# A two-layer streaming trunk on one core: the router of the second layer chooses before the norm's factor is known, the first gather is handed over in halves, the dense FFN waits by banks, and fifteen short products are added

## The chip, the cores and the metric

The kernel runs on one core of a Trainium2 chip. The metric is the device time of one execution in microseconds (us). TensorE multiplies, VectorE (DVE) and ScalarE (ACT) work element by element and prepare its operands, GpSimd (POOL) takes a small part in the recurrence, and SyncE (SP) issues nearly all DMAs.

## The reference

A trunk of two layers over 16 learned tokens and 256 frames of width 1024. Each layer runs three mixers in parallel on one projection, gates and merges them, multiplies by `w_out` and adds to the stream. Then comes an FFN on the normed stream: dense in layer 0, eight experts in layer 1.

```python
h = h + merged @ w_out[i]
hn = rms_norm(h, norm_ffn[i])
if i % 2 == 0:
    h = h + swiglu(hn, dense_w_gate[j], dense_w_up[j], dense_w_down[j])
else:
    h = h + moe_swiglu(hn, moe_router[j], moe_w_gate[j], moe_w_up[j], moe_w_down[j])

def moe_swiglu(x, router, wg, wu, wd):
    logits = (x @ router).astype(jnp.float32)
    top_val, top_idx = lax.top_k(logits, TOP_K)
    top_w = jax.nn.softmax(top_val, axis=-1)
    gates = jnp.sum(jax.nn.one_hot(top_idx, N_EXPERTS, dtype=jnp.float32) * top_w[..., None], axis=-2)
    y = jnp.zeros_like(x)
    for e in range(N_EXPERTS):
        y = y + gates[..., e:e + 1].astype(x.dtype) * swiglu(x, wg[e], wu[e], wd[e])
    return y
```

`rms_norm` divides each token's row by the root of its mean square. That factor is one positive number for all of a token's logits, so it doesn't change which two are largest; it scales their difference.

## The kernel before

**Layout and precision.** The stream is held transposed in `hT`, eight tiles of 128 features by T = 272 tokens. Most products are made in three parts: both operands are split into a high part, rounded to fp32r, and a low part, the difference. `three_products` (L538 to L540) adds high by high, low by high and high by low. ScalarE makes the high part of each half chunk of weights (`high_half`, L1350; `expert_high`, L1691: WH from ring), VectorE the low part (`low_half` and `expert_low`: WL, through the helper at L1776, which is the line of all its two-operand instructions). There are three buffers of each, used in turn. TensorE waits on `w_lo` for a half and counts it in `w_used` when done; ScalarE waits on `w_used` before it overwrites a buffer. SyncE loads chunks of 2 MB into a ring of three as `w_lo` frees them (`expert_loads`, L424).

**Order on the engines.** Each engine walks through a fixed list of halves. `split_stage` calls the splitting of a half and then the events that are written down for that place by `after_half(events, l, name, half)`. An engine carries out its list strictly in order, so an event that waits holds back the splits behind it.

**Norms.** `norm` on TensorE (L612) multiplies a matrix of ones by the squares, in three parts of 4, 2 and 2 feature tiles (`PARTS`), which ScalarE squares (L1355). VectorE makes the mean (L1790), ScalarE the root, VectorE the reciprocal (L1792) and the scaled `xn` (L1794). `keep_clock` (L603) issues ten products that nobody reads meanwhile.

**Dense FFN of layer 0.** Two blocks of hidden chunks, 0 to 3 and 4 to 6. For each chunk a gate product goes to PSUM banks 0 to 3 (`DG`) and an up product to banks 4 to 7 (`DU`). VectorE reads the gate banks into SF (`gate_scaled`, counts `f_g`) and the up banks into HF (`hidden`, counts `f_h`); after the block the down products (`DD`, `rows_half`) go to banks 0 to 7 and VectorE adds them to `hT` (`down`, `added`, L1776).

**From `w_out` to the experts.** The last two chunks of layer 1 before the experts are `O0` and `O1`, for banks 0 to 3 and 4 to 7, each in two halves (`columns_half`). VectorE adds the banks to `hT` (`added`), and makes the router's input in three parts: `router_input` (L1809) multiplies by the norm's gain alone. Between the halves of `O1` TensorE does part 0 of the sum of squares and `router_part(0)`: logits (L657) and transposes of the tokens (L663). After `O1` come the other parts. The reciprocal root is in a row; two products with one column turn it (L1189). Ten unread products follow (L1192). VectorE scales the logits (L2233), takes the two largest (`max`, `max_index`), makes one-hot rows of them (L2245), TensorE ranks the tokens for each expert (L1195 to L1199), VectorE makes slots (L2255, L2256) and the selection matrix of the first expert (L2373). ScalarE copies the turned tokens, scaled, into `hnT` (L1700), and makes the exponential for the gate weights (L1703). `gather` (L1207) multiplies the tokens by the selection, ScalarE copies the result into XGH (L1707), VectorE makes XGL from it, and `half_products` starts with the first half of the first expert. Each expert has 42 halves in a loop. The order is kept by the semaphores `router_pe`, `router_dve` and `router_act`, whose counts `ROUTER` names.

## Time and profile before

| | us |
|---|---|
| median of three runs | 2135.67 (2133.98 to 2139.07) |
| the profiled execution | 2132.18 |
| its span, first to last instruction | 2130.2 |
| TensorE busy | 2071.9 (97%) |
| VectorE busy | 1479.6 (69%) |
| ScalarE busy | 1230.9 (58%) |
| mean granted TensorE clock | 0.995 of full speed |

The stages in the trace: layer 0 up to about 380 us, its dense FFN up to 686, layer 1 up to 1106, the router up to 1125, the experts up to 2104, the last norm and the output. Durations of single instructions overlap on TensorE, because products are pipelined; what one costs in a stream is the time of many divided by their number. A full-precision product appears as two records, a rounded one (fp32r) as one.

### The profile page before, as it was taken

What the parts mean: (1) busy time and instruction counts of PE and PEld (TensorE: products, weight loads), DVE (VectorE), ACT (ScalarE), POOL (GpSimd) and SP (SyncE); (2) the same over time, 40 slices, a digit from 0 to 9 for tenths busy, and PEclk for the clock granted to TensorE, in tenths of its full rate; (3) what the DMA queues carried; (4) which work ended last, traced back from release to release, by engine and by line L of the source; (5) the groups of instructions that cost most, each with busy time, mean ns of one, the idle gap of its engine ahead of it and who ended that gap; (6) DMA issues with size and microseconds to landing.
All of it is one profiled execution on the core that took longest, in us unless ns stands there. A gap on an engine that the chain in (4) does not pass through costs nothing.

```text
span 2130.2 us, 35940 instructions
## 1 busy us (share of the span) xinstructions
PE 2071.9 (97%) x15200; PEld 1799.0 (84%) x15200; DVE 1479.6 (69%) x1340; ACT 1230.9 (58%) x1147; POOL 22.1 (1%) x24
## 2 busy tenths in 40 slices
PE   9999999999999999999999999999999999999997
PEld 7877789999999797788997888888888888888886
DVE  5633438565454673434848889898898989899886
ACT  4455445443333455445437777777777777777675
POOL 0000100000000000010000000000000000000000
PEclk9999999999999999999999999999999999999999
DMA  6323105444443232210637989899898989989894
GB/s 240 129 63 139 57 3 198 158 184 173 158 180 120 80 122 96 80 42 10 240 119 302 374 331 375 347 359 365 338 371 330 374 348 359 366 339 370 331 372 173
DMA packets 73981, 485.38 MB, mean 228 GB/s; under 512 B 12440, under 2 KB 13592, under 8 KB 16136
## 3 DMA queue, kind: packets, MB, share of 16 engines
q1 hardware_dynamic: 72584, 479.96, 58.3%
q10 hardware_dynamic: 1280, 3.70, 0.5%
q8 instruction: 94, 1.54, 0.3%
q14 instruction: 23, 0.19, 0.0%
HBM read 481.89 MB, written 1.74 MB: 227 GB/s over the span
## 4 chain that ended last, share of the span: by engine, by line
PE 91%; DVE 5%; ACT 2%; issue 1%; DVEq 0%; ACTq 0%
PE PS L538 24%; PE PS L540 23%; PE PS L539 23%; PE PS L943 5%; PE PS L809 2%; DVE area L1776 2%; PE PS L827 2%; PE PS L1207 1%; PE PS L1214 1%; PE PS L688 1%; DVE WL L1776 1%; PE PS L851 1%; ACT WH L1691 1%; PE PS L890 1%; PE PS L796 0%
## 5 line engine op out<-in xcount | busy, mean ns | idle before, releaser
L1776 DVE TENSOR_TENSOR WL<-ring,WH 128x2048 fp32r<-128x2048 f32 x410 | 934.2, 2289 | 218.1 <-ACT WH L1350 111.9
L1691 ACT ACTIVATE WH<-ring 128x2048 fp32r<-128x2048 f32 x336 | 643.0, 1916 | 156.9 <-PE PS L540 156.9
L538 PE MATMUL PS<-WH,XGH 128*128 128x512 f32 x896 | 353.5, 395 | 2.4 <-DVE XGL L1776 2.4
L540 PE MATMUL PS<-WL,XGH 128*128 128x512 f32 x896 | 349.6, 390 | 0.0
L539 PE MATMUL PS<-WH,XGL 128*128 128x512 f32 x896 | 349.1, 390 | 0.0
L540 PE MATMUL PS<-XL,WH 128*128 128x272 f32 (+1 forms) x704 | 202.6, 288 | 0.0
L1350 ACT ACTIVATE WH<-ring 128x2048 fp32r<-128x2048 f32 x74 | 141.1, 1910 | 104.3 <-PE PS L540 104.2
L538 PEld LDWEIGHTS PS<-WH,XGH 128*128 128x128 f32 x896 | 168.3, 188 | 36.3 <-DVE XGL L1776 2.6
L540 PEld LDWEIGHTS PS<-WL,XGH 128*128 128x128 f32 x896 | 168.2, 188 | 35.7
L539 PEld LDWEIGHTS PS<-WH,XGL 128*128 128x128 f32 x896 | 168.4, 188 | 33.5
L538 PE MATMUL PS<-WH,HTH 128*128 128x512 f32 x448 | 176.5, 394 | 0.6
L540 PE MATMUL PS<-WL,HTH 128*128 128x512 f32 x448 | 174.6, 390 | 0.0
L539 PE MATMUL PS<-WH,HTL 128*128 128x512 f32 x448 | 174.4, 389 | 0.0
L943 PE MATMUL PS<-area 64*64 64x64 f32 (+1 forms) x3680 | 129.1, 224 | 12.5 <-DVE area L1776 9.3
L943 PEld LDWEIGHTS PS<-area 64*64 64x64 f32 x3680 | 120.1, 135 | 20.3 <-DVE area L1776 13.6
L540 PEld LDWEIGHTS PS<-XL,WH 128*128 128x128 f32 x704 | 132.3, 188 | 0.0
L538 PE MATMUL PS<-FXH,WH 128*128 128x272 f32 x448 | 129.3, 289 | 2.3 <-DVE hT L1776 1.5
L539 PE MATMUL PS<-FXH,WL 128*128 128x272 f32 x448 | 128.8, 287 | 0.0
L1776 DVE TENSOR_TENSOR area<-PS,cst 128x256 f32<-128x256 f32 (+2 forms) x78 | 30.2, 404 | 122.6 <-PE PS L856 61.6
L538 PE MATMUL PS<-XH,WH 128*128 128x272 f32 (+1 forms) x384 | 109.7, 286 | 0.9 <-DVE ML L1776 0.4
L539 PE MATMUL PS<-XH,WL 128*128 128x272 f32 (+1 forms) x384 | 109.1, 284 | 0.0
L538 PEld LDWEIGHTS PS<-WH,HTH 128*128 128x128 f32 x448 | 84.1, 188 | 20.4 <-issue 3.7
(350 smaller groups left out, 3526.7 us busy)
## 6 DMA issues: line engine op xcount, KB each, us to landing
ring<-in_experts SPq DMA_DIRECT2D x336, 1024.0 KB, 6.6
ring<-in_weights SPq DMA_DIRECT2D x114, 1024.0 KB, 6.8
ring<-in_weights SPq DMA_DIRECT2D x4, 576.0 KB, 6.3
ring<-in_weights SPq DMA_DIRECT2D x4, 512.0 KB, 4.1
cst<-in_consts ACTq DMA_DIRECT2D x1, 1731.0 KB, 8.2
area<-in_x ACTq DMA_DIRECT2D x2, 512.0 KB, 4.7
out<-area SPq DMA_DIRECT2D x4, 256.0 KB, 2.1
bias_line<-lin SPq DMA_DIRECT2D x1, 672.0 KB
```

The lines of the kernel that those rows point to most:

```text
L538: pe.matmul(o, lh, rh, start=first, stop=False, skip_group_check=True)
L539: pe.matmul(o, ll, rh, start=False, stop=False, skip_group_check=True)
L540: return pe.matmul(o, lh, rl, start=False, stop=last, skip_group_check=True)
L688: ins = pe.matmul(PS[0:m, t % 4, 0:T], chunk_bufs[name][:, k, c:c + m], xn[:, k, 1:T + 1], start=(k == 0), stop=(k == KT - 1))
L809: ins = pe.matmul(PS[:, 6 + i % 2, 0:T], window_bufs[0][:, k, c:c + P], xn[:, k, 1:T + 1], start=(k == 0), stop=(k == KT - 1))
L827: ins = pe.matmul(PS[:, gate_bank(n), lo:T], early_bufs[0][:, k, (n % 4) * P:(n % 4 + 1) * P], xn[:, k, 1 + lo:T + 1], start=(k == 0), sto ...
L851: mm = lambda o, a, b_: pe.matmul(o, a, b_, start=False, stop=False, skip_group_check=True)
L890: ins = pe.matmul(PS[0:m, g, o:o + n], lhs, kC[r:r + 64, t0:t0 + n], start=True, stop=True)
L943: ins = pe.matmul(PS[r, bank, n * p + col:n * p + col + n], lhs[r, p], rhs(r, p), start=start if first is None else first and p == 0, stop ...
L1350: act.activation(WH[(g + 1) % 3][:, :], ring[b][:, 2048 * (g % 2):2048 * (g % 2) + 2048], ACT.Copy).then_inc(S("w_hi"), 1)
L1691: act.activation(WH[(BASE + j + 1) % 3][:, :], ring[b][:, 2048 * (j % 2):2048 * (j % 2) + 2048], ACT.Copy).then_inc(S("w_hi"), 1)
L1776: tt = lambda o, a_, b_, op: dve.tensor_tensor(o, a_, b_, op)
```

## The change

- **Short products.** In layer 1's first norm, ahead of the third part of the sum of squares, fifteen products of rounded operands (left from the dense FFN) with 96, 192 and 128 columns, five of each. Nobody reads their result.
- **Dense FFN.** The first down product of a block waits for `f_g` (banks 0 to 3 read), and only ahead of bank 4 for `f_h` (banks 4 to 7 read). The sum of the first block into `hT` starts with banks 0 to 3 on `f_mid`, which is counted after bank 3 of the block's last half.
- **Router.** The logits are compared unscaled. The squares are summed per token, as weights against one column of ones, so the mean is in a column without a turn. The order on TensorE is logits, squares, transposes by parts. The factor enters later, in the difference of the two largest logits. The ten unread products become two and three.
- **Splits.** The first two halves of the first expert are split under the halves of `O1`; the fill of the slots too.
- **First gather.** After its first four feature tiles TensorE counts `router_pe`; ScalarE and VectorE split the gathered tokens in two halves, and TensorE starts the first expert half, which needs only the first. Each expert's other products wait for `e_xgl` at their top.

`expert_high` and `expert_low` are moved up unchanged. In the diff line numbers are left out.

```diff
-        ROUTER = {"logits": 1, "turned": 2, "squares": 3, "rank": 4, "rstd": 1, "selected": 2, "gap": 3, "rows": 1, "exp": 2}
+        ROUTER = {"logits": 1, "squares": 2, "turned": 3, "rank": 4, "gathered": 5,
+                  "mean": 1, "selected": 2, "rstd": 3, "gap": 4, "rows_low": 5,
+                  "root": 1, "rows": 2, "exp": 3, "rows_high": 4}
...
             def norm(l, which, parts=(0, 1, 2), spare_products=10):
                 for i in parts:
+                    if (l, which, i) == (1, 0, 2):
+                        for n in (96, 192, 128):
+                            for _ in range(5):
+                                pe.matmul(PS[:, 1, 256:256 + n], FHH[:, 1, 0:P], FHH[:, 0, 0:n], start=True, stop=True)
                     if (l, which, i) == (0, 0, 0):
...
-            def router_part(q):
-
-                for i in PARTS_OF[q]:
-                    pe.wait_ge(S("hg_done"), i + 4)
...
+            def token_block(t):
+
+                return slice(META + t * P, META + (t + 1) * P)
+
+            def router_logits(i):
+
+                pe.wait_ge(S("hg_done"), i + 4)
+                for k in range(*PARTS[i]):
                     for t in range(2):
                         ins = pe.matmul(PS[:, 1, 8 * t:8 * t + 8], xn[:, k, 1 + META + t * P:1 + META + (t + 1) * P], router_sb[:, k, :],
                                         start=(k == 0 and t == 0), stop=(k == KT - 1), skip_group_check=True)
-                if q:
-                    ins.then_inc(S("router_pe"), 1)
+                return ins
+
+            def router_squares(i):
+
+                pe.wait_ge(S("sq_done"), part(DEPTH - 1, 1, i))
+                for k in range(*PARTS[i]):
+                    for t in range(2):
+                        ins = pe.matmul(PS[:, 0, t:t + 1], squares_of(DEPTH - 1, 1)[:, k, token_block(t)], C("ones", 0, 1),
+                                        start=(k == 0 and t == 0), stop=(k == KT - 1), skip_group_check=True)
+                return ins
...
+            def router_turns(i):
+
                 for t in range(2):
...
+                    for k in range(*PARTS[i]):
+                        ins = pe.transpose(PS[:, 2 + t + 2 * (k // 4), (k % 4) * P:(k % 4 + 1) * P],
+                                           xn[:, k, 1 + META + t * P:1 + META + (t + 1) * P], C("ident"))
+                return ins
...
                         if l and (h, half) == (1, 0):
-                            norm(l, 1, (0,))
-                            router_part(0)
-                if l:
-                    norm(l, 1, (1, 2), 0)
+                            router_logits(0)
+                            router_squares(0)
+                            router_turns(0)
...
                             pe.wait_ge(S("f_lo"), f + 1)
                             if f == block[0]:
-                                pe.wait_ge(S("f_h"), block[-1] + 1)
+                                pe.wait_ge(S("f_g"), block[-1] + 1)
+
+                            def before(d_):
+
+                                if f == block[0] and d_ == 4:
+                                    pe.wait_ge(S("f_h"), block[-1] + 1)
+
                             for half in range(2):
                                 q0 = 4 * (f - block[0])
                                 rows_half(l, f"DD{f}", half, 0, lambda k: FHH[:, q0 + k, :], lambda k: FHL[:, q0 + k, :],
-                                          f == block[0] and half == 0, f == block[-1] and half == 1, None,
-                                          *(("f_mid", "f_late") if f == FG - 1 and half else (None, None)))
-
-            router_part(1)
-            pe.wait_ge(S("ms_done"), 4)
-            for t in range(2):
-                ins = pe.matmul(PS[:, 7, t:t + 1], rstd[0:1, META + t * P:META + (t + 1) * P], C("ones")[0:1, 0:1], start=True, stop=True)
-            ins.then_inc(S("router_pe"), 1)
-            for _ in range(10):
-                pe.matmul(PS[:, 0, 0:2 * P], C("ones"), cst[:, 0:2 * P], start=True, stop=True)
+                                          f == block[0] and half == 0, f == block[-1] and half == 1, None if half else before,
+                                          "f_mid" if f == block[-1] and half else None, "f_late" if f == FG - 1 and half else None)
...
+            def unread(count):
+
+                for _ in range(count):
+                    pe.matmul(PS[:, 7, 0:2 * P], C("ones"), cst[:, 0:2 * P], start=True, stop=True)
+
+            router_logits(1)
+            router_turns(1)
+            router_squares(1)
+            router_logits(2).then_inc(S("router_pe"), 1)
+            router_squares(2).then_inc(S("router_pe"), 1)
+            router_turns(2).then_inc(S("router_pe"), 1)
+            unread(2)
             pe.wait_ge(S("router_dve"), ROUTER["selected"])
...
+            unread(3)
             pe.wait_ge(S("router_act"), ROUTER["rows"])
...
-            def gather(wait_for):
+            def gather(wait_for, mid=None):
 
                 pe.wait_ge(S("e_sel"), wait_for)
                 for k in range(KT):
                     for t in range(2):
                         ins = pe.matmul(PS[:, 2 + k // 4, (k % 4) * SLOTS:(k % 4 + 1) * SLOTS], hnT[:, t, k * P:(k + 1) * P],
                                         SEL[:, t, :], start=(t == 0), stop=(t == 1))
+                    if mid and k == 3:
+                        ins.then_inc(S(mid), 1)
                 ins.then_inc(S("e_xg"), 1)
...
             def expert_products(pe, e, n, run, last):
+                pe.wait_ge(S("e_xgl"), n + 1)
                 for j in range(1, HALVES):
...
+                if isinstance(run, int) and run == 0:
+
+                    gather(1, "router_pe")
+                    pe.wait_ge(S("router_dve"), ROUTER["rows_low"])
+                else:
+                    gather(run * NE + 1)
+                    pe.wait_ge(S("e_xgl"), run * NE + 1)
                 half_products(run * NE, 0)
...
                 after_half(events, l, "O0", 1).append((square, l, 1, 0))
+                if l:
+                    for j in range(2):
+                        after_half(events, l, f"O{j}", 1 - j).append((expert_high, 0, j))
...
-            act.wait_ge(S("router_pe"), ROUTER["squares"])
-            act.activation(MR[:, 184:186], PS[:, 7, 0:2], ACT.Sqrt).then_inc(S("rt_done"), 1)
-            expert_high(0, 0)
+            act.wait_ge(S("router_dve"), ROUTER["mean"])
+            act.activation(MR[:, 184:186], MR[:, 184:186], ACT.Sqrt).then_inc(S("router_act"), 1)
             act.wait_ge(S("router_pe"), ROUTER["turned"])
             act.wait_ge(S("router_dve"), ROUTER["rstd"])
...
-                for j in range(0 if run else 1, 3):
+                first = isinstance(run, int) and run == 0
+                for j in range(2 if first else 0, 3):
                     expert_high(run * NE, j)
-                gathered_high(act, run * NE + 1)
+                if first:
+                    act.wait_ge(S("router_pe"), ROUTER["gathered"])
+                    act.activation(XGH[:, 0:512], PS[:, 2, :], ACT.Copy).then_inc(S("router_act"), 1)
+                    act.wait_ge(S("e_xg"), 1)
+                    act.activation(XGH[:, 512:D], PS[:, 3, :], ACT.Copy).then_inc(S("e_xgh"), 1)
+                else:
+                    gathered_high(act, run * NE + 1)
...
+            def slot_pads():
+
+                dve.memset(MR[:, 64:82], -1.0)
...
                     after_half(events, l, "O0", 1).append((router_input, 0))
+                    after_half(events, l, "O0", 1).append((expert_low, 0, 0))
+                    after_half(events, l, "O1", 0).append((expert_low, 0, 1))
+                    after_half(events, l, "O1", 0).append((slot_pads,))
...
-                        dve.wait_ge(S("w_used"), split_half[(0, f"DD{last}")] + 2)
+                        if h:
+                            dve.wait_ge(S("w_used"), split_half[(0, f"DD{last}")] + 2)
+                        else:
+                            dve.wait_ge(S("f_mid"), 1)
                         tt(hT[:, q, :], hT[:, q, :], PS[:, q, 0:T], ALU.add).then_inc(S("f_acc"), 1)
                         dve.wait_ge(S("f_acc"), h + 1)
...
                         after_half(events, l, f"DD{DENSE_BLOCKS[0][-1]}", 1).append((down, DENSE_BLOCKS[0][-1], h))
                     last = f"DD{FG - 1}"
-                    after_half(events, l, last, 1).append((added, 0, "f_mid", 1))
+                    after_half(events, l, last, 1).append((added, 0, "f_mid", len(DENSE_BLOCKS)))
...
-            dve.wait_ge(S("sum_done"), 4)
-            dve.tensor_scalar(rstd[:, META:], PS[:, 0, META:T], 1.0 / D, EPS, ALU.mult, ALU.add).then_inc(S("ms_done"), 1)
-            dve.memset(MR[:, 64:82], -1.0)
-            dve.wait_ge(S("rt_done"), 4)
-            dve.reciprocal(MR[:, 184:186], MR[:, 184:186]).then_inc(S("router_dve"), 1)
-            dve.wait_ge(S("router_dve"), ROUTER["rstd"])
             dve.wait_ge(S("router_pe"), ROUTER["logits"])
             idx = MR[:, 96:112].bitcast(U32)
-            for t in range(2):
-                ins = dve.tensor_scalar(MR[:, 8 * t:8 * t + 8], PS[:, 1, 8 * t:8 * t + 8], MR[:, 184 + t:185 + t], None, ALU.mult)
-            v(ins)
+            v(dve.tensor_scalar(MR[:, 0:16], PS[:, 1, 0:16], 1.0, None, ALU.mult))
...
+            dve.wait_ge(S("router_pe"), ROUTER["squares"])
+            dve.tensor_scalar(MR[:, 184:186], PS[:, 0, 0:2], 1.0 / D, EPS, ALU.mult, ALU.add).then_inc(S("router_dve"), 1)
             v(dve.tensor_copy(MR[:, 128:144], idx))
...
+            dve.wait_ge(S("router_act"), ROUTER["root"])
+            dve.reciprocal(MR[:, 184:186], MR[:, 184:186]).then_inc(S("router_dve"), 1)
+            dve.wait_ge(S("router_dve"), ROUTER["rstd"])
             for t in range(2):
-                ins = tt(MR[:, 176 + t:177 + t], MR[:, 113 + 8 * t:114 + 8 * t], MR[:, 112 + 8 * t:113 + 8 * t], ALU.subtract)
+                ins = dve.tensor_scalar(MR[:, 176 + t:177 + t], MR[:, 113 + 8 * t:114 + 8 * t], MR[:, 112 + 8 * t:113 + 8 * t],
+                                        MR[:, 184 + t:185 + t], ALU.subtract, ALU.mult)
...
                 select_next(S("e_sel"))
-                expert_low(run * NE, 0)
-                if isinstance(run, int) and run == 0:
+                first = isinstance(run, int) and run == 0
+                if first:
                     gate_weights()
-                gathered_low(run * NE + 1)
-                for j in range(1, AHEAD):
+                    dve.wait_ge(S("router_act"), ROUTER["rows_high"])
+                    tt(XGL[:, 0:512], PS[:, 2, :], XGH[:, 0:512].bitcast(F32), ALU.subtract).then_inc(S("router_dve"), 1)
+                    dve.wait_ge(S("e_xgh"), 1)
+                    tt(XGL[:, 512:D], PS[:, 3, :], XGH[:, 512:D].bitcast(F32), ALU.subtract).then_inc(S("e_xgl"), 1)
+                else:
+                    expert_low(run * NE, 0)
+                    gathered_low(run * NE + 1)
+                for j in range(2 if first else 1, AHEAD):
                     expert_low(run * NE, j)
```

## Rows read from the trace of the kernel before

**Rows 1.** The page, part 1: busy time and share of the span of each engine.

```profile
PE 2071.9 (97%) x15200; PEld 1799.0 (84%) x15200; DVE 1479.6 (69%) x1340; ACT 1230.9 (58%) x1147; POOL 22.1 (1%) x24
```

**Rows 2.** TensorE's waits, whole run: us in total, times, longest.

```profile
PE PS L538 <- issue: 4.5, 8, 1.4
```

**Rows 3.** The chain that ended last, router: start, us, what.

```profile
1108.55 1.68 PE PS L657 x16
...
1111.69 4.51 PE PS L1192 x20
...
1118.77 3.82 PE PS L1207 x32
...
1122.61 1.03 ACT XGH L1707
...
1123.74 1.24 DVE XGL L1776
...
1125.02 0.50 PE PS L538
```

**Rows 4.** Windows: us, busy PE, PEld, DVE, ACT, POOL, PE clock, DMA share, GB/s.

```profile
524.60:574.50 49.90, 48.45 (x384) 48.26 (x384) 20.92 (x10) 16.35 (x9) 0.00 (x0) 1.00 0.45 169
...
728.60:735.40 6.80, 6.43 (x19) 5.02 (x20) 6.00 (x9) 1.94 (x5) 0.00 (x0) 0.51 0.45 188
...
776.40:779.80 3.40, 3.40 (x18) 3.40 (x17) 3.33 (x6) 0.13 (x1) 0.00 (x0) 0.53 0.00 0
...
1095.80:1100.20 4.40, 4.40 (x34) 4.09 (x34) 0.00 (x0) 0.00 (x0) 0.00 (x0) 1.00 0.01 6
...
1100.20:1105.90 5.70, 5.70 (x50) 5.70 (x49) 1.31 (x3) 0.66 (x1) 0.00 (x0) 1.00 0.00 0
...
1125.00:1250.60 125.60, 125.42 (x582) 103.53 (x583) 110.03 (x70) 90.79 (x60) 0.00 (x0) 1.00 0.90 353
```

**Rows 5.** The chain that ended last, at three places of the dense FFN.

```profile
524.60 1.42 issue
...
574.51 1.30 DVE hT L1776
...
575.94 0.36 PE PS L538
...
648.65 1.43 issue
```

**Rows 6.** Timeline of VectorE, dense FFN: start, duration, instruction, idle before.

```profile
512.56 1.29 DVE L1776 TENSOR_TENSOR area<-PS,rstd 128x1088 f32<-128x1088 f32 x1 [1.78 <-PE PS L540]
...
524.63 1.29 DVE L1776 TENSOR_TENSOR area<-area,PS 128x1088 f32<-128x1088 f32 x1 [1.71 <-PE PS L540]
...
570.43 2.29 DVE L1776 TENSOR_TENSOR WL<-ring,WH 128x2048 fp32r<-128x2048 f32 x1 [3.63 <-ACT WH L1350]
```

**Rows 7.** The chain that ended last, layer 1's first norm.

```profile
686.38 3.68 PE PS L612 x16
...
692.91 1.75 DVE xn L1794 x4
```

**Rows 8.** Timeline of ScalarE, layer 1's first norm and router.

```profile
687.17 0.66 ACT L1355 ACTIVATE area<-hT 128x544 f32<-128x544 f32 x1 [0.79 <-DVE hT L1776]
...
1113.61 2.41 ACT L1700 ACTIVATE area<-PS,area 128x512 f32<-128x512 f32 x4
...
1117.44 3.69 ACT L1691 ACTIVATE WH<-ring 128x2048 fp32r<-128x2048 f32 x2
```

**Rows 9.** Timeline of VectorE, router.

```profile
1112.13 0.36 DVE L2233 TENSOR_SCALAR area<-PS,area 128x8 f32<-128x8 f32 x2
...
1114.08 0.38 DVE L1776 TENSOR_TENSOR area<-area 128x8 f32<-128x8 f32 x4
...
1120.74 0.16 DVE L2262 TENSOR_SCALAR area<-area 128x2 f32<-128x2 f32 x1
...
1122.59 0.15 DVE L2270 TENSOR_SCALAR small<-small 128x1 int32<-128x1 f32 x1
```

More of the change, by code:

```diff
@@ L649, in _ @@
                 ins.then_inc(S("in_turned"), 1)
-            def router_part(q):
-                for i in PARTS_OF[q]:
-                    pe.wait_ge(S("hg_done"), i + 4)
-                for k in range(4 * q, 4 * q + 4):
+            def token_block(t):
[3 more added lines that the diff above has]
+                for k in range(*PARTS[i]):
                     for t in range(2):
@@ L658, in router_part @@
                                         start=(k == 0 and t == 0), stop=(k == KT - 1), skip_group_check=True)
-                if q:
-                    ins.then_inc(S("router_pe"), 1)
-                for t in range(2):
-                    for k in range(4):
-                        ins = pe.transpose(PS[:, 2 + t + 2 * q, k * P:(k + 1) * P],
-                                           xn[:, 4 * q + k, 1 + META + t * P:1 + META + (t + 1) * P], C("ident"))
-                if q:
-                    ins.then_inc(S("router_pe"), 1)
+                return ins
[7 more added lines that the diff above has]
+            def router_turns(i):
+                for t in range(2):
+                    for k in range(*PARTS[i]):
+                        ins = pe.transpose(PS[:, 2 + t + 2 * (k // 4), (k % 4) * P:(k % 4 + 1) * P],
+                                           xn[:, k, 1 + META + t * P:1 + META + (t + 1) * P], C("ident"))
+                return ins
             for l in range(DEPTH):
@@ L1277, in first_gather @@
                     scatter()
-                gather(run * NE + 1)
-                pe.wait_ge(S("e_xgl"), run * NE + 1)
+                if isinstance(run, int) and run == 0:
[4 more added lines that the diff above has]
+                    pe.wait_ge(S("e_xgl"), run * NE + 1)
                 half_products(run * NE, 0)
@@ L1350, in high_half, with expert_high @@
                 act.activation(WH[(g + 1) % 3][:, :], ring[b][:, 2048 * (g % 2):2048 * (g % 2) + 2048], ACT.Copy).then_inc(S("w_hi"), 1)
+            def expert_high(n, j):
+                b = (MOE0 + j // 2) % RING
+                if j % 2 == 0:
+                    act.wait_ge(S(f"landed{b}"), n * (32 * PER_BUF) + (landed_moe0[b] + 32 * (j // 2 // RING + 1)))
+                act.wait_ge(S("w_used"), n * HALVES + (j - 2 + BASE))
+                act.activation(WH[(BASE + j + 1) % 3][:, :], ring[b][:, 2048 * (j % 2):2048 * (j % 2) + 2048], ACT.Copy).then_inc(S("w_hi"), 1)
             def square(l, which, i):
@@ L1786, in low_half, with expert_low @@
                    WH[(g + 1) % 3][:, :].bitcast(F32), ALU.subtract).then_inc(S("w_lo"), 1)
+            def expert_low(n, j):
+                half = j % 2
+                dve.wait_ge(S("w_hi"), n * HALVES + (j + 1 + BASE))
+                tt(WL[(BASE + j + 1) % 3][:, :], ring[(MOE0 + j // 2) % RING][:, 2048 * half:2048 * half + 2048],
+                   WH[(BASE + j + 1) % 3][:, :].bitcast(F32), ALU.subtract).then_inc(S("w_lo"), 1)
             def norm(l, which, gain):
@@ L2278, in v_e @@
                 dve.wait_ge(S("e_chain"), wait_for)
-            def expert_low(n, j):
-                half = j % 2
-                dve.wait_ge(S("w_hi"), n * HALVES + (j + 1 + BASE))
-                tt(WL[(BASE + j + 1) % 3][:, :], ring[(MOE0 + j // 2) % RING][:, 2048 * half:2048 * half + 2048],
-                   WH[(BASE + j + 1) % 3][:, :].bitcast(F32), ALU.subtract).then_inc(S("w_lo"), 1)
             def add_expert(i):
```

7 lines of the change are left out of this document (removed).

## The prediction

> **What bounds the kernel now.** I read the page first: TensorE is busy in 97% of a span of 2130.2 us [rows 1]. The table of waits then says where it stood still; the line to see is that of the down and up products, eight waits of 4.5 us with none over 1.4 [rows 2]. The table is not enough for the router, because TensorE also spends time there on products that nobody reads, so for that stretch I read the chain of waits, which counts them [rows 3]. Once the experts run, TensorE is busy for 125.42 of 125.60 us [rows 4], so that stage is paced by TensorE and whatever comes earlier moves the end by as much. The same row shows DMA at 0.90; that is close, but leaves TensorE no gap, so I let it be.
>
> **Dense waits by banks.** Three stalls are addressed. The first down product of each block waits until VectorE has made the last hidden values, 1.29 us from 524.63; TensorE stands from 524.60 for 1.42 us [rows 5, 6]. After the change the down products into banks 0 to 3 wait only for the earlier read of those banks, 512.56 to 513.85 [rows 6], and only bank 4 waits for the 1.29 us. 384 products take 48.45 us in this stage, 0.126 each [rows 4]; four banks of a half are 24 products, 3.0 us, which covers it. Saved: 1.42 us of standing, and the restart, since the first product after a pause takes 0.36 instead of 0.13 us [rows 5]: 1.65. The second block has the same stall, 1.43 us [rows 5], again 1.65. Between the blocks VectorE's sum into hT waits for the whole half (574.51), and TensorE for the first part of that sum, until 575.94 [rows 5]. Now the first part may start when banks 0 to 3 are finished, 3.0 us earlier at 571.5; VectorE is in a split of weights until 570.43 + 2.29 = 572.72 [rows 6], then sums for 1.30 and ends at 574.0, half a microsecond before TensorE wants the banks. Saved: 1.47 us (1.30 and the hand-overs on both sides) and the restart, 1.7. Nothing is late next: the split that VectorE does afterwards is for a half that starts a whole half, 6 us, later. Dense together 5.0 us; at least 3.5 if the half microsecond of cover is missing and one release costs a microsecond, at most 5.2.
>
> **The short products.** Fifteen products of 96, 192 and 128 columns, 2080 columns in all, go in front of the third part of layer 1's sum of squares. Nothing hides them: the sum runs as 16 records in 3.68 us without a gap [rows 7], the squares of its third part were ready at 687.83 [rows 8], and TensorE gets there at 689.1. The sum is on the path (it, the root, the reciprocal and the first scaled inputs, up to 692.91 + 1.75 [rows 7], then the first projection), so their whole time is added. The ten spare products behind the sum start later too and still end before the projection. No rounded product under 256 columns is in this trace. Bounds: one pass at 256 columns takes 5.70 us for 50, 0.114 each [rows 4], so 2080 columns cost at least 0.93 us; a full-precision product of 272 columns is two records of 0.23 [rows 7], 1.69 ns a column, so 3.5 us, and with 128 columns two of 0.119 (3.82 us for 32 [rows 3]), which makes up to 3.9. I take 3.5, because by columns the nearest rows are the full-precision ones of 128, and every rounded one here has 256 or more.
> The 8-column products of the router take 1.68 us for 16 records, 0.105 each [rows 3], although they stream almost nothing. The Trainium skill (TensorE: Matmul & The Clock Gate, section LDWEIGHTS) says that loading 128 weight columns takes 128/1.2 GHz, some 107 ns, whatever the rest. By that rule the trace agrees, and an estimate from it is 15 x 0.107 = 1.6 us if the short products stay single-pass.
>
> **The router, before.** From the last product of w_out (1105.9) to the first expert product (1125.02) pass 19.1 us. In the chain stand logits 1.68, unread products 4.51 up to 1116.20, gather 3.82, its high part 1.03, its low part 1.24 [rows 3]; VectorE had made the choice by 1114.3, in the middle of the row at 1114.08 [rows 9].
>
> **The router, after.** Part 0, inside w_out's last half: 16 records with one column (0.105 each, 1.68 us) instead of 8 with 272 (1.84): w_out ends at 1105.75. Behind it come logits of part 1 (8 records, 0.84), four transposes (0.48, by the gather's records), squares (0.84), logits of part 2 (0.84): complete at 1108.75. The inputs of part 2 are there at 1107.1: a sum of 0.7 and scaling of 0.6 on VectorE behind w_out. From logits to choice VectorE took 1112.13 to 1114.3 [rows 9]; it has one scaling less and one mean more now, 2.1 us: chosen at 1110.9. TensorE does squares 0.84, transposes 0.48, two unread 0.90 and is free at 1110.95. From there to the gather it was 1116.20 to 1118.77, 2.57 us [rows 3], for rank products, ranks and selection: 1113.5; the three unread products (1.35) end by then. ScalarE: the mean and root are early, the reciprocal comes behind the choice at 1111.15, the four scaled copies take 2.41 [rows 8]: rows ready at 1113.6. This is last by a little, so the gather starts at 1113.75, its first half is done at 1115.7, the whole at 1117.6. On ScalarE the exponential with its table load (1.4 us, between 1113.61 + 2.41 and 1117.44) and a split of 1.85 [rows 8] stand in front, so the first half's copy starts at 1116.9 and ends at 1117.5 (half of 1.03 and a start-up). VectorE has 2.0 us of gate weights (1120.74 to 1122.74 [rows 9]) from 1115.1 to 1117.1, then the low half, 0.69, to 1118.2. The second halves end at 1118.9 under the first expert half, 12 products of 0.23. First product at 1118.2 instead of 1125.02: 6.8 us. Bounds: 5.3 if two releases or the order on ScalarE cost 1.5 us more, 7.8 if the split does not delay the copy.
>
> **Edits at nothing.** The first two expert splits move under w_out's last halves, where VectorE and ScalarE stand: busy 0.00 in one window, 1.31 and 0.66 of 5.70 us in the next [rows 4], for 3.8 and 4.6 us of work. Behind ScalarE's wait for the freed weight buffer are queued the other squares, wanted at 1103.8, and behind VectorE's the sums into hT, wanted at 1103.1, for which TensorE waits; the splits end by 1097.7 and 1100.1. Without that cover what sticks out would delay w_out's tail, up to 4.5 us. The loads of the fourth expert chunk (two DMAs on SP, nothing behind them but later loads) go out at 1100 instead of 1127, into empty queues (share 0.00 [rows 4]). The wait at the top of each expert's products is met long before: 0 to 0.14 us (a hand-over) each, eight times, at most 1.1. I take 0.
>
> **Sum.** -5.0 + 3.5 - 6.8 = -8.3 us. The profiled execution took 2132.18 us, 2.0 more than its span, and would take 2123.9. The median shown is 2135.67, 3.5 above it, so I forecast 2127.4.
>
> **Rivals.** (a) The forecast: 0.45.
> (b) Short products stay single-pass at the pace of a weight load, 15 of 0.105 us by [rows 3], 1.6 us: sum -10.2, 2125.5. For it: a rate that columns don't set is seen; against it: no rounded row below 256 columns. 0.25. It is where the skill's rule would lead.
> (c) The half gather brings little, because ScalarE's split and VectorE's gate weights stand in front of it, and the chain to the choice is slower than added up: the router gives half, 3.4 us: sum -4.9, 2130.8. For it: both engines work in order, and the split ends 1.2 us after the first half of the gather. 0.14.
> (d) The banks don't help, since another input of the first down product is late; -1.7 instead of -5.0: sum -5.0, 2130.7. Against: every other input was there. 0.06.
> (e) The other side, TensorE's clock. The granted clock is 0.51 from 728.6 to 735.4 and 0.53 from 776.4 to 779.8 [rows 4]: 10.2 us at 1.2 GHz, which cost up to 5.1. In the first of them TensorE ran products of few rows with pauses. What lies ahead may move or multiply such stretches. A microsecond at 1.2 GHz costs 0.5, so 16.6 us more of it cancel the gain and 25 make the kernel 0.2% slower, 2140. 0.10. They may as well fall away, worth 5.1, which bounds the low end.
>
> **Numbers.** 0.2% is 4.3 us and about what a measurement of this kernel can tell from no change: faster is below 2131.4, slower above 2139.9. (a) and (b) are nearly all faster (0.68 of 0.70), (c) and (d) lie close to the bound (0.12 of 0.20 faster, the rest the same), (e) is split: 0.04 slower, 0.03 same, 0.03 faster. Faster 0.83, same 0.13, slower 0.04. The range: -11.9 with all bounds good, -4.9 with all bad, and about 1.5 for the spread of the runs: 2122.3 to 2132.3.
>
> **What would show it.** No pause between the last up and the first down product of either block, none at the second block's first gate product; the short products as 15 records of some 0.1 us (b) or dearer (a), and layer 1's sum longer by just that; 12.4 us from w_out's last product to the first expert product, with ScalarE's four copies as the last releaser of the gather and VectorE's low half as that of the first product. The forecast fails if the short products lie outside 0.9 to 3.9 us, if the experts' stage takes longer, or if the granted clock is low over a longer stretch.

## The result and the profile after

The changed kernel takes 2120.98 us (median of five runs, 2119.65 to 2124.0), the kernel before beside it 2139.07 (five runs, 2133.98 to 2143.69). The ratio is 0.992, interval 0.9901 to 0.994: 0.8% faster, where 0.4% was forecast. 2127.4 us and the range down to 2122.3 were both too slow. In later batches 57 more runs of the kernel before (one of 10.6 ms left out) have a median of 2136.9, so 2 of the 18 us between the medians are chance; some 16 have to be explained, 8.3 were forecast. The two profiled executions lie 11.2 us apart (2132.18 and 2120.98); the profiled one of before was one of its fastest.

The page of the changed kernel, part 1, answers to [rows 1]:

```profile
PE 2072.7 (98%) x15217; PEld 1800.0 (85%) x15217; DVE 1480.4 (70%) x1340; ACT 1231.4 (58%) x1148; POOL 22.0 (1%) x24
```

TensorE works as long as before; what went is time in which it stood. The waits of the changed kernel and one window, against [rows 2] and the first of [rows 4]:

```profile
PE PS L540 <- issue: 1.6, 6, 0.3
```

```profile
524.60:574.50 49.90, 49.90 (x400) 49.90 (x400) 23.37 (x12) 17.61 (x10) 0.00 (x0) 1.00 0.48 180
...
1094.30:1099.50 5.20, 5.20 (x43) 5.20 (x42) 3.21 (x3) 1.91 (x1) 0.00 (x0) 0.84 0.00 2
1099.50:1106.00 6.50, 6.50 (x51) 6.50 (x50) 1.31 (x3) 0.66 (x1) 0.00 (x0) 0.86 0.89 325
1106.00:1118.40 12.40, 11.71 (x93) 10.60 (x92) 7.40 (x38) 8.85 (x12) 0.00 (x0) 1.00 0.00 1
```

In the dense stage TensorE now makes 400 products in the time of 384, without a gap; between 500 and 690 us the table of its waits is empty, so the three stalls of [rows 5] are gone. The first norm of layer 1 in the chain, against [rows 7]:

```profile
681.69 2.75 PE PS L618 x12
684.44 1.62 PE PS L612 x15
686.06 0.98 PE PS L618 x4
...
689.89 1.75 DVE xn L1847 x4
```

The sum of squares starts 4.7 us earlier than before, and the fifteen products cost 1.62 us. What is left of that, 3.0 us at the end of the norm, is lost again in layer 1. From the norm's last scaled input to the end of w_out, in the kernel before and then in the changed one:

```profile
694.66:1105.90 411.24, 394.27 (x4189) 346.36 (x4190) 221.23 (x317) 194.52 (x291) 10.92 (x10) 0.99 0.27 102
```

```profile
691.64:1106.00 414.36, 397.68 (x4199) 349.66 (x4199) 225.86 (x320) 198.25 (x293) 10.92 (x10) 0.98 0.29 106
```

The second stretch is 3.1 us longer and has 17.1 us at the lower clock level (1.2 GHz) where the first has 10.2. So w_out ends at the same time in both traces, 1105.9 and 1106.0. The router, against [rows 3]; L666, L675 and L683 are logits, squares and transposes, L1740 the scaled copies, L1743 the exponential, L1789 the copy of the gather's first half:

```profile
1106.00 0.79 PE PS L666 x8
...
1108.07 0.90 PE PS L666 x8
...
1111.90 1.84 ACT area L1740 x3
...
1113.76 1.28 ACT L1743
...
1115.26 1.80 ACT WH L1396
1117.06 0.49 ACT XGH L1789
...
1117.64 0.70 DVE XGL L1823
```

The first expert product starts at 1118.38, 12.4 us behind w_out, as worked out; two other executions with that router at full clock have 12.4 us too (1113.62 to 1126.02 in the router alone, 1110.83 to 1123.22 in the kernel with the groups of twelve, both below). The chain runs over ScalarE: copies, table load, the split of the third expert half, then the copy of the half gather. The gather itself started on the selection, not on ScalarE's copies as the forecast had it:

```profile
1114.04 3.81 PE L1237 MATMUL PS<-area 128*128 128x128 f32 x32 [0.16 <-DVE area L2428]
```

What the forecast did not have is in the last stage, behind the last expert product. The chain of the kernel before, and then that of the changed one (L1293 and L1331 are the same transposes of the stream, L1299 and L1337 the same sums of the last expert):

```profile
2112.39 4.49 issue
2116.88 3.02 PE PS L1293 x16
2119.91 2.20 PE PS L1299 x7
```

```profile
2106.43 1.08 issue
2107.51 1.94 PE PS L1331 x16
2109.44 1.63 PE PS L1337 x7
```

"issue" is time in which TensorE stands and no other engine's work explains it. This pause, right behind the loop over the experts, is 3.4 us shorter, and the same products behind it take 3.57 instead of 5.22 us. The whole stage has 12.8 instead of 17.8 us:

```profile
2106.40:2119.20 12.80, 3.82 (x25) 3.12 (x24) 4.47 (x8) 3.59 (x7) 0.00 (x0) 0.84 0.22 85
```

```profile
2112.40:2130.20 17.80, 5.43 (x24) 4.60 (x24) 4.47 (x8) 3.59 (x7) 0.00 (x0) 0.74 0.16 61
```

### The profile page after: what moved, and what is told of

It is laid out like the page before. It is cut to its first block, busy times and chain, and to the rows that moved or that the text cites. A ratio compares the mean times of both kernels' runs of the same rounds, so it can differ in the third digit from the quotient of the medians.

```text
span 2119.2 us, 35975 instructions
## 1 busy us (share of the span) xinstructions
PE 2072.7 (98%) x15217; PEld 1800.0 (85%) x15217; DVE 1480.4 (70%) x1340; ACT 1231.4 (58%) x1148; POOL 22.0 (1%) x24
## 3 DMA queue, kind: packets, MB, share of 16 engines
q8 instruction: 94, 1.54, 0.3%
## 4 chain that ended last, share of the span: by engine, by line
PE 92%; DVE 5%; ACT 3%; issue 1%; DVEq 0%; ACTq 0%
PE PS L540 24%; PE PS L542 23%; PE PS L541 23%; PE PS L962 5%; PE PS L828 2%; PE PS L846 2%; DVE area L1823 2%; PE PS L1237 1%; PE PS L1246 1%; PE PS L707 1%; DVE WL L1823 1%; PE PS L870 1%; ACT WH L1396 1%; PE PS L909 1%; PE PS L815 0%
```

## The experiments

Each run lists its mean granted clock, and time and clock go together: over the 57 runs of the kernel before the clock lies between 0.988 and 0.996 and the time between 2147 and 2132 us. Two numbers are worked out from that for each kernel. The time at the lower level (1.2 GHz) is twice what the mean clock lacks of 1, times the run's time; the time at full clock is the run's time less half of that. The second is an estimate, since the lower level costs nothing while TensorE stands. Over the 57 runs it brings the standard deviation from 3.7 to 1.2 us; in the small groups it doesn't always help (dense waits alone 1.7 and 1.8). The clock is listed to three places, and half a step of the last one is 1 us of time, so differences of a microsecond in the last column can't be trusted. Each ratio is to the runs of the kernel before that were made beside that row.

| kernel | runs | median us | ratio to before, interval | at 1.2 GHz, mean us | at full clock, mean us |
|---|---|---|---|---|---|
| before, beside all of these | 57 | 2136.9 | | 28.8 | 2123.8 |
| before again, as a kernel of its own | 8 | 2139.0 | 1.0023 [1.0013, 1.0034] | 33.7 | 2122.9 |
| short products alone | 11 | 2136.9 | 0.9995 [0.9979, 1.001] | 27.2 | 2122.4 |
| dense waits alone | 11 | 2132.9 | 0.9984 [0.9974, 0.9994] | 29.1 | 2118.4 |
| router alone | 5 | 2125.5 | 0.9952 [0.9938, 0.9966] | 23.0 | 2114.4 |
| changed kernel | 5 | 2121.0 | 0.992 [0.9901, 0.994] | 22.9 | 2109.8 |
| changed, without the fifteen | 6 | 2120.1 | 0.9913 [0.9889, 0.9937] | 24.7 | 2108.2 |
| the same, another order | 6 | 2119.4 | 0.9905 [0.9883, 0.9927] | 22.6 | 2107.8 |
| changed, gather handed over whole | 5 | 2123.6 | 0.9935 [0.9917, 0.9954] | 22.9 | 2112.8 |
| before, 15 products more | 12 | 2132.4 | 0.9972 [0.9958, 0.9987] | 23.8 | 2121.2 |
| before, two unread products | 12 | 2133.7 | 0.999 [0.9975, 1.0005] | 29.6 | 2121.1 |

The second row shows what a ratio is worth here: the same kernel, 1.0023 with an interval that leaves out 1.

**The kernel before again.** No edit.

> The kernel before, unchanged, for what it does by itself. The forecast missed because the change brought 18 us between the medians and 11 between the two profiled executions; the router and the dense part came as forecast. Theory L (code layout): the last stage of the kernel before always has TensorE standing 4.5 us ahead of the last transposes (line 1293), because its next code arrives late, followed by a stretch at the lower clock, and the changed kernel has 1.1 us there. Then this profile shows the 4.5 us again. Theory C (clock in layer 1): the medians differ by more than the profiles because the kernel before has longer stretches of granted clock 0.5 in most runs; then the runs' clocks lie between 0.990 and 0.995 and the time falls with them, some 5 us per 10 us of low clock, and the 4.5 us is as often small. Time ratio to the kernel before 1.000 by either.

Its last stage has the pause again:

```profile
2116.58 4.58 issue
2121.16 3.35 PE PS L1293 x16
```

So the pause belongs to the kernel (theory L), and the stretches of low clock vary from run to run (theory C has a part: this execution has 6.8 us of it in the router, where that of [rows 3] has none, and there its ten unread products take 6.29 instead of 4.51 us).

**The short products alone.** The four lines of the diff's first hunk, in the kernel before.

> The kernel before with the fifteen short products alone. By the records of the changed kernel they cost 15 x 0.108 = 1.62 us (not 3.5). If they are only a cost: +1.6 us, ratio 1.0008, and the last stage keeps its 4.5 us. If their instructions shift TensorE's code against the blocks in which it is loaded (theory L), the pause ahead of the last transposes changes, up to -5 us. If they settle the clock in layer 1 (theory C), the low stretches there shrink from 10 us and the spread of the runs gets smaller: -2 to -8 us.

```profile
2122.03 1.36 issue
2123.40 1.94 PE PS L1297 x16
```

The pause is short. At full clock the kernel gains 1.4 us, give or take 1.2; 1.6 paid and 3.1 got from the pause would be 1.5. The clock was no steadier: 27.2 us at the lower level against 28.8, runs from 2130.5 to 2143.9. In the medians nothing can be told.

**The dense waits alone.** All edits of the diff that name `f_g`, `f_h` or `f_mid`.

> The kernel before with the dense waits by banks alone (both waits of TensorE and the earlier sum). From the two traces: 4.7 us less up to layer 1's norm, ratio 0.9978, if nothing is given back. Theory C says that the later stretches of low clock move with it, so the time could be between -10 and 0; theory L says that the pause in the last stage stays 4.5 us, since no instruction of TensorE was added (the number is nearly the same).

5.4 us less at full clock, 4.0 between medians; 4.1 up to the norm in its profile. The pause is 4.49 us.

**The router alone.** The changed kernel with those edits undone and without the fifteen products.

> The changed kernel without the fifteen products and with the dense waits as before: the router's part alone. From the last product of w_out to the first expert product 12.4 instead of 19.1 us, so -6.7 us, ratio 0.9969. Theory L: the pause in the last stage is small here too (TensorE's code before it has other lengths), which makes -11 to -12 us in all, ratio 0.9945. Theory C: the pause stays and the time is about -6.7 with a spread like that of the kernel before.

11.4 us less between medians, 9.4 at full clock; the pause is 1.13 us and the last stage 12.8. So the router's part brings its 6.7 us and, by where it puts the code behind it, the last stage.

**Without the fifteen.**

```diff
-                    if (l, which, i) == (1, 0, 2):
-                        for n in (96, 192, 128):
-                            for _ in range(5):
-                                pe.matmul(PS[:, 1, 256:256 + n], FHH[:, 1, 0:P], FHH[:, 0, 0:n], start=True, stop=True)
```

> The changed kernel without the fifteen short products. Theory L: the router's part alone already brought the last stage's pause down to 1.1 us, so the fifteen have nothing left to shift, and without them the pause stays at 1.1 to 1.4 us and the time falls by their own 1.6 us: 2119.4 against the 2121.0 of the changed kernel, ratio to the kernel before some 0.991 to 0.992. Theory C: they help the clock, so without them the low stretches grow from some 23 us to those of the kernel before, 27, and the time is 2121 or above.

The pause stays short (1.5 us), and next to the router's part the fifteen products are a cost: 1.62 us in the traces. At full clock the kernel without them takes 1.6 us less, between medians 0.9; neither difference is clear of the spread of five and six runs. Its profile has the lower level for most of the router, which the changed kernel's has not:

```profile
1104.00:1116.00 12.00, 12.00 (x56) 11.10 (x56) 5.31 (x34) 6.48 (x9) 0.00 (x0) 0.57 0.00 1
```

One execution each can't tell whether the products do that. The run with another order, also without them, has 10.2 us of the lower level in its router too, the run with the gather handed over whole, with them, has none; but that with 60 warm-up products, with them, has 10.2. Over the runs the difference is 1.8 us at the lower level, 0.9 us of time, which is no more than the listed clock can tell.

**Fifteen products, nothing else.** In the kernel before:

```diff
-            for _ in range(12):
-                pe.matmul(PS[:, 7, 0:2 * P], rstd[:, 0:P], rstd[:, 0:2 * P], start=True, stop=True)
+            for _ in range(27):
+                pe.matmul(PS[:, 7, 0:96], rstd[:, 0:P], rstd[:, 0:96], start=True, stop=True)
```

> The kernel before with fifteen instructions more at the very start of TensorE's program and nothing else: the warm-up has 27 products of 96 columns in place of 12 of 256, as long within a microsecond. Theory L (where TensorE's code lies against the blocks in which it is loaded): the pause ahead of the last transposes falls from 4.5 to 1.4 us as with the fifteen short products, the low clock behind it shrinks too, last stage 13 instead of 17.8 us, time -5 us, ratio 0.9977. If the pause depends on something else that the short products did, it stays 4.5 us and the ratio is 1.000.

What the expectation counts as one instruction is one product in full precision, in the trace two weight loads and two matmul records. The pause is 1.1 us, the last stage 12.8 us, and the kernel 0.28% faster (2.6 us at full clock), by a warm-up cut finer, with a first norm that came 0.9 us later.

**The price by columns.** Six groups of twelve products of 16, 96, 128, 192, 256 and 384 columns in place of the fifteen; L611 to L621 in that order, in the chain:

> The changed kernel with twelve products each of 16, 96, 128, 192, 256 and 384 columns in place of the fifteen, for the price of a rounded product by columns. If they are one pass at the pace of a weight load (0.105 us by the 8-column rows): 0.107 each for 16 to 256 columns and 0.165 at 384, so groups of 1.3 us and one of 2.0. If short ones fell back to four passes: 0.16, 0.21 and 0.32 at 96, 128 and 192.

```profile
684.94 1.24 PE PS L611 x12
686.18 1.38 PE PS L613 x12
687.56 1.35 PE PS L615 x12
688.91 1.38 PE PS L617 x12
690.29 1.40 PE PS L619 x12
691.69 2.08 PE PS L621 x12
```

0.113 to 0.117 each from 96 to 256 columns, 0.173 at 384. The 1.24 us is the chain's share of the first group and lacks part of a product; by their starts its products lie 0.112 us apart. In the groups of 96, 128 and 192 columns the weight loads start 0.112 us apart, whatever the columns: one pass, paced by the load of 128 weight columns.

**Another order in the first gather**, on top of the kernel without the fifteen:

```diff
-                for j in range(2 if first else 0, 3):
+                for j in range(0 if not first else 3, 3):
                     expert_high(run * NE, j)
...
                     act.activation(XGH[:, 0:512], PS[:, 2, :], ACT.Copy).then_inc(S("router_act"), 1)
+                    expert_high(0, 2)
...
-                    gate_weights()
                     dve.wait_ge(S("router_act"), ROUTER["rows_high"])
                     tt(XGL[:, 0:512], PS[:, 2, :], XGH[:, 0:512].bitcast(F32), ALU.subtract).then_inc(S("router_dve"), 1)
+                    gate_weights()
```

> The changed kernel without the fifteen, and with another order in the first gather: ScalarE copies the first half as soon as TensorE has counted it and splits the third expert half only then, VectorE makes the low half before the gate weights. The price of what stood in front of the half gather. By the trace of the changed kernel the copy could start at 1116.1 instead of 1116.96, and the first expert product at 1117.4 instead of 1118.4: -1.0 us against the run without the fifteen; if the third half's low part is late then (wanted 5.6 us after the start), up to 0.5 us of it comes back.

0.4 us at full clock, 0.7 between medians, against the run without the fifteen: not told from nothing. ScalarE now stands ready for 4.27 us, and it is the gather that it waits for:

```profile
1117.06 0.60 ACT L1785 ACTIVATE XGH<-PS 128x512 fp32r<-128x512 f32 x1 [4.27 <-PE PS L1233]
```

In this execution the gather lay in a stretch at the lower level, which covers what the order could give. It is the fastest version by its median, 0.95% below the kernel before, though not shown faster than the changed kernel.

**One product more.** In the kernel before, 13 warm-up products of 236 columns instead of 12 of 256.

> The kernel before with one instruction more at the start of TensorE's program (13 warm-up products of 236 columns instead of 12 of 256). Counting TensorE's instructions in program order, the last transposes (line 1293) are number 10112 in the kernel before and with the dense waits alone, both with a pause of 4.5 us, and 10113 in the router's part alone, with 1.1 us. 10112 is a multiple of 64. Theory L64: the pause is long when these products begin exactly at such a multiple, right behind the branch that TensorE lands on. Then one instruction more brings the pause to some 1.1 us. If it is the length of the code and not the place, one instruction does nothing: 4.5 us.

```profile
2115.16 1.11 issue
2116.27 1.94 PE PS L1293 x16
```

One product more at the far end of the program removes 3.4 us of pause; the last stage is 12.8 us. Its single run took 2129.75 us, less than any of the 57.

**Forty-eight products more in the changed kernel.** 60 warm-up products of 16 columns.

> The changed kernel with 48 instructions more at the start of TensorE's program (60 warm-up products of 16 columns instead of 12 of 256, which also cost some 5 us there; only the last stage is read). Its last transposes move from number 10128 to 10176, again a multiple of 64. Theory L64: the pause ahead of them grows from 1.1 to 4.5 us and the last stage from 12.8 to some 17.7 us, so that this part of the gain belongs to no part of the change's purpose. Otherwise it stays 1.1.

```profile
2131.90 1.35 issue
2133.25 1.72 PE PS L1331 x14
2134.97 1.82 issue
2136.80 0.38 PE PS L1331 x2
```

A pause is back, but a second one, behind 14 of the 16 transposes, 3.2 us together instead of 4.5. The place of the code decides; that it decides by multiples of 64 in that count is refuted.

**Two unread products instead of ten** in the kernel before, with eight more products in the warm-up (20 of 144 columns).

> The kernel before with two unread products instead of ten behind the turned root, and eight instructions more at the start (20 warm-up products of 144 columns instead of 12 of 256), so that the last transposes keep their place and the pause its 4.5 us. In the chain the ten take 4.51 us and end at 1116.20, the choice is there at 1114.3: if the chain is right, -1.9 us, ratio 0.9991. If the ten keep the clock up, the stretch to the first expert product shows more of the lower level and nothing is gained.

The number of products ahead of the last stage is that of the kernel before, though the warm-up is another, and the pause is 4.41 us: it goes with the number, not with what the warm-up looks like. At full clock the kernel takes 2.7 us less, with the time at the lower level hardly changed (29.6 us against 28.8), ratio 0.999, interval 0.9975 to 1.0005. In the profile the selection is ready 1.5 us after the ranks as before, but the gather, 3.82 us in [rows 3], comes in a stretch at the lower level:

```profile
1115.21 6.62 PE PS L1207 x32
```

```profile
1110.00:1114.00 4.00, 2.03 (x14) 1.51 (x12) 2.52 (x21) 4.00 (x5) 0.00 (x0) 1.00 0.01 2
1114.00:1122.00 8.00, 6.60 (x32) 6.44 (x32) 4.80 (x16) 5.25 (x6) 0.00 (x0) 0.57 0.00 0
```

Ahead of it TensorE was busy for 2.03 of 4 us. From w_out's end to the gather 11.3 us pass instead of 12.9, so the ten are on the path and cost 1.6 us there. That they keep the clock up is not shown. With all ten in place the gather takes 5.45 us in the profiles of the dense waits alone and of the fifteen and the one more in the warm-up, 3.82 in the others, and in the kernel before again and the short products alone the ten themselves lie at the lower level (6.29 and 6.54 us). The changed kernel's five, spread over two gaps, left 0.69 us without work in 12.4.

**The gather handed over whole.** In the changed kernel, `gathered_high` and `gathered_low` for the first expert too.

> The changed kernel with the first gather handed over whole, as before: one copy on ScalarE, one low part on VectorE. What the halves are worth. By the changed kernel's trace the gather ends at 1117.85; copy 1.03 and low part 1.24 with their hand-overs bring the first expert product to 1120.2 instead of 1118.4, +1.8 us, ratio to the changed kernel 1.0009. If the halves bring nothing (rival c), within 0.3 us.

```profile
1118.43 3.82 PE PS L1237 x32
...
1122.28 1.03 ACT XGH L1742
...
1123.40 1.24 DVE XGL L1812
```

From the gather's start to the low part's end 6.21 us, in the changed kernel 4.30 (1114.04 to 1118.34): 1.9 us, as expected. Between medians it is 2.6, at full clock 3.0; the rest is spread.

## Why the prediction was wrong

**What bounds the kernel: right for the experts, and no further.** The experts' stage took 987.4 and 988.0 us (1125.02 to 2112.39, 1118.38 to 2106.43). The wait at the top of each expert cost nothing that shows: the profiles without it have 987.4 to 989.8 us, those with it 987.5 to 988.3. That "whatever comes earlier moves the end by as much" holds through that stage and fails behind it. It also failed ahead of it, in layer 1, where the profiled pair lost 3.1 us to the clock.

**Dense waits: right.** Forecast 5.0; up to the norm 4.7 in the changed kernel's trace and 4.1 in that of the dense waits alone, 5.4 at full clock alone. Rival (d) falls: the three stalls are gone.

**Short products: mis-sized.** Forecast 3.5, measured 1.62. The step that failed is the choice "because by columns the nearest rows are the full-precision ones of 128". The better neighbour was the 8-column row: up to 256 columns the products follow each other at the pace of the weight loads, 0.112 to 0.117 us, and columns set the price only at 384. Rival (b) holds, 0.108 each. The Trainium skill (TensorE: Matmul & The Clock Gate, section LDWEIGHTS) gives a load of 128 weight columns some 107 ns. The measured pace is 5 to 9% above that.

**Router: right.** Forecast 6.8; 19.1 became 12.4 us. Choice, copies, gather and first product came within 0.3 us of the times worked out; the selection came 0.5 us later than "1113.5", so that it, and not ScalarE's four copies, released the gather. That the absolute times fit is luck in part: they were counted from a w_out that ends at 1105.75, without what the dense stage saved, and the clock in layer 1 had eaten that. Counted from w_out's end they fit by themselves. Rival (c) falls: the half gather alone is worth 1.9 us.

**Edits at nothing: this is where the forecast failed.** They were costed by what they do to the engines' work, and the experts' stage was the last thing that the sum looked at. The last stage stands in no term, which puts it at nothing, while the change shifts its code. It went from 17.8 to 12.8 us. That is no accident of the pair: the four profiles with a long pause (kernel before twice, dense waits alone, two unread) have 17.7 to 19.0 us there, the nine with a short one 12.8 to 13.2.

In the long pause three transfers of the instruction queues lie. The kernel before, from the pause's start over its length:

```profile
q8 instruction: 1, 0.02, 1.3%
q14 instruction: 2, 0.02, 1.1%
```

They don't tell a long pause from a short one. The same 4.5 us of the changed kernel (2106.43 to 2110.92), in most of which TensorE works, have the same three:

```profile
q14 instruction: 2, 0.02, 1.3%
q8 instruction: 1, 0.02, 1.3%
```

In all executions one 16 KB transfer of q8 starts 0.8 to 1.5 us ahead of the pause and one 1.6 to 2.3 us behind its start. q8 goes with TensorE's instructions: five transfers from 930 to 955 us, where TensorE ran 728 matmuls, none from 1300 to 1325, inside the loop over the experts. What differs is which of the two the work follows. Times in us from the pause's start, by the packets in the traces:

| execution | q8 transfer that ends last ahead of the work | it ends | TensorE goes on | later by |
|---|---|---|---|---|
| changed kernel | first | -0.46 | 1.08 | 1.54 |
| short products alone | first | -0.19 | 1.36 | 1.55 |
| without the fifteen | first | -0.06 | 1.49 | 1.55 |
| before | second | 3.01 | 4.49 | 1.48 |
| before again | second | 3.18 | 4.58 | 1.40 |
| dense waits alone | second | 3.13 | 4.49 | 1.36 |
| two unread products | second | 2.91 | 4.41 | 1.50 |
| forty-eight more, its second pause | second | 3.40 | 4.90 | 1.50 |

The other short pauses end 1.53 to 1.72 us behind the end of the first. So a short pause goes with the end of the first transfer, and a long one with the end of the second. Shown by runs is that the pause depends on how many products TensorE has ahead of that place, one being enough. That TensorE waits for the q8 load is read from these times and no run sets it by itself; where the boundaries of the loads lie stays open.

**The clock: a smaller part, and not all of it placed.** Rival (e) priced it mainly as a loss. It did name a gain of up to 5.1 us "which bounds the low end", but the range was added up without it: with it the low end would have lain below the measured 2120.98. (The good bounds of the three terms add up to -12.1, not -11.9, which changes nothing.) Behind the long pause the products run in part at the lower level: 9.2 us of the last stage in the profiled kernel before, 6.7, 12.0 and 6.6 in the three others with the long pause, 3.1 to 5.7 in those with the short one. The 23 records of transposes and sums take 5.0 to 6.4 us behind a long pause and 3.6 behind a short one, on average 1.9 us more. Over all runs the changed kernel has 22.9 us at the lower level, the kernel before 28.8: 3.0 us of time, of which these 1.9 are placed. In the profiled pair it is the other way round, 21.3 against 19.4 us, because of layer 1.

**The sum.** The profiled pair adds up: -3.0 up to the norm's end (-4.7 dense, +1.6 short products), +3.1 in layer 1, -6.7 in the router, +0.7 in the experts, -5.1 in the last stage, together -11.0 us of span. For the medians: -4.7 - 6.7 + 1.6 - 3.4 (pause) = -13.2 us at full clock, where -14.0 was measured; with -3.0 for the clock -16.2, where the medians give -15.9 (2136.9 to 2121.0). Of the 7.6 us by which the forecast of -8.3 missed, the last stage is 5.2 (the average of the profiles, pause 3.3 and products 1.9), the short products 1.9. What is left is within the 2.1 us by which the kernel before differed from itself.

What the fifteen products are good for: in the kernel before they remove the pause; next to the router's edits, which already shift the code, nothing is left for them. A steadier clock is not shown.

## What to carry to other kernels

Read the stage behind a change too, also where no line of it is touched: an "issue" pause behind a loop can come and go with one product 2115 us ahead, so measure an edit with a neutral product or two beside it before its effect is put down to what it does. When a sign is found in a long pause, look for it in as long a window of the kernel without the pause. Price a short product by its weight load, not by its columns. When unread products on the path are removed, look at the granted clock of what follows, and in more than one execution: with and without them it was low in some.

## What the runs showed of the hardware

One product more at the start moved a pause 2115 us later from 4.5 to 1.1 us, and the pause ended 1.4 to 1.7 us behind the end of a 16 KB transfer of instructions in all fourteen executions. A rounded product costs 0.11 to 0.12 us from 16 up to 256 columns and 0.173 at 384. The mean granted clock of one kernel on one core varies between 0.988 and 0.996 from run to run, and with it the time by 15 us; most of the spread of these runs is that.
